# Modulation in eight contraction chunks, with seven projection blocks run on each chunk and their sums kept in SBUF, in a one-step hybrid decoder layer

## The reference, cut to what matters

```python
mod = c @ w_ada + b_ada                      # w_ada: 4096 x 12288
shift, scale, gate = jnp.split(mod, 3, axis=-1)
h = _rmsnorm(x, g_norm) * (1.0 + scale[:, None]) + shift[:, None]
proj = h @ w_in                              # w_in: 4096 x 10240
a_b, a_c, a_x, a_g, b_x, b_g, c_u, c_g = _split_cols(proj)
# A: gated convolution of 3, B: convolution of 4 and RG-LRU, C: complex S5, GELU and GLU
mixed = jnp.concatenate([out_a, out_b, out_c], axis=-1) @ w_out
x = x + gate[:, None] * mixed                # then a final RMSNorm of x
```

## Time and profile before

| what | us |
|---|---|
| median of 3 runs | 2138.58 (2137.79 to 2139.91) |
| the profiled execution | 2137.69 |
| its span, first to last instruction | 2136.1 |
| TensorE busy | 2007.3 (94%) |
| VectorE, ScalarE, POOL busy | 1051.4, 800.7, 434.3 |
| mean granted TensorE clock | 0.986 of 2.4 GHz |
| read from HBM, written | 463.09 MB, 10.07 MB |

### The profile page before, as it was taken

How to read it: one execution, slowest core, us unless ns; L and a number is a source line. 1 busy time by engine, 2 the same in 40 slices (tenths; PEclk the granted TensorE clock), 3 DMA queues, 4 the chain that set the end, 5 groups by cost and what they waited for, 6 DMA issues and landing times.

```text
span 2136.1 us, 36787 instructions
## 1 busy us (share of the span) xinstructions
PE 2007.3 (94%) x13066; PEld 1724.2 (81%) x13066; DVE 1051.4 (49%) x1324; ACT 800.7 (37%) x1075; POOL 434.3 (20%) x501
## 2 busy tenths in 40 slices
PE   2887999999999998999989999999999999999994
PEld 0111777778999997989979999999988888888883
DVE  4812233233447677676777455565653333333334
ACT  3001223233334444444435445646563323333232
POOL 0000000000107765867658101000000000000001
PEclk9999999999999999999999999999999999999997
DMA  7999999997543433334333444454457787666862
GB/s 311 410 410 385 334 339 348 344 332 291 172 144 127 133 127 117 129 120 141 123 126 130 161 147 165 134 173 154 155 216 259 261 318 258 249 247 246 306 234 98
DMA packets 129149, 473.88 MB, mean 222 GB/s; under 512 B 14640, under 2 KB 15472, under 8 KB 128960
## 3 DMA queue, kind: packets, MB, share of 16 engines
q1 hardware_dynamic: 122256, 445.70, 58.1%
q0 software_dynamic: 4816, 18.10, 2.5%
q10 hardware_dynamic: 2016, 9.42, 1.1%
HBM read 463.09 MB, written 10.07 MB: 222 GB/s over the span
## 4 chain that ended last, share of the span: by engine, by line
PE 74%; POOL 7%; DMA 7%; issue 5%; DVE 4%; ACTq 1%; ACT 1%; POOLq 0%; SPq 0%; DVEq 0%
PE m L375 22%; PE m L377 21%; PE m L376 21%; DMA ada_ring<-in_ada 6%; PE aux L393 4%; PE aux L499 3%; POOL s_tmpp L1260 1%; POOL s_tmpp L1257 1%; PE aux L481 1%; DVE x L1184 1%; POOL cos L1218 1%; POOL s_h__105 L1256 1%; POOL sin L1216 1%; DMA ada_ring_x<-in_ada 1%; DVE w_lo L833 1%
## 5 line engine op out<-in xcount | busy, mean ns | idle before, releaser
L375 PE MATMUL m<-h_hi,w_hi 128*128 128x320 f32 x3584 | 1131.8, 316 | 4.7 <-DVE w_lo L833 4.6
L377 PE MATMUL m<-h_hi,w_lo 128*128 128x320 f32 x3584 | 1109.4, 310 | 0.0
L376 PE MATMUL m<-h_lo,w_hi 128*128 128x320 f32 x3584 | 1109.0, 309 | 0.0
L833 DVE TENSOR_TENSOR w_lo<-w_raw,w_hi 128x1024 fp32r<-128x1024 f32 x456 | 577.4, 1278 | 838.4 <-ACT w_hi L529 837.3
L529 ACT ACTIVATE w_hi<-w_raw 128x1024 fp32r<-128x1024 f32 x456 | 478.9, 1056 | 903.2 <-PE m L377 577.5
L375 PEld LDWEIGHTS m<-h_hi,w_hi 128*128 128x128 f32 x3584 | 674.9, 188 | 130.9 <-issue 113.6
L376 PEld LDWEIGHTS m<-h_lo,w_hi 128*128 128x128 f32 x3584 | 675.5, 188 | 0.8
L377 PEld LDWEIGHTS m<-h_hi,w_lo 128*128 128x128 f32 x3584 | 675.0, 188 | 0.0
L393 PE MATMUL aux<-ada_ring,c_T 128*32 128x512 f32 x512 | 123.8, 620 | 24.3 <-DMA ada_ring<-in_ada 24.3
L393 PEld LDWEIGHTS aux<-ada_ring,c_T 128*32 128x32 f32 x512 | 17.7, 110 | 124.2 <-DMA ada_ring<-in_ada 120.1
L393 PE MATMUL aux<-ada_ring_x,c_T 128*32 128x512 f32 x512 | 70.8, 612 | 3.6 <-DMA ada_ring_x<-in_ada 3.6
(11 more groups left out here) (237 smaller groups left out, 1507.6 us busy)
## 6 DMA issues: line engine op xcount, KB each, us to landing
w_raw<-in_w SPq DMA_DIRECT2D x456, 512.0 KB, 4.3
ada_ring<-in_ada SPq DMA_DIRECT2D x128, 512.0 KB, 9.0
ada_ring_x<-in_ada SPq DMA_DIRECT2D x128, 512.0 KB, 5.9
gate_ring<-in_ada SPq DMA_DIRECT2D x128, 512.0 KB, 5.7
x<-in_x ACTq DMA_DIRECT2D x1, 5120.0 KB, 16.6
x<-in_x POOLq DMA_DIRECT2D x8, 640.0 KB, 5.3
out_y<-x SPq DMA_DIRECT2D x7, 640.0 KB, 3.0
part_b<-part_b POOLq DMA_DIRECT2D x4, 688.0 KB, 6.5
```

The lines of the kernel that those rows point to most:

```text
L375: mm(out, w_hi, hi[:, k, :], start=k == k0, stop=False)
L376: mm(out, w_hi, lo[:, k, :], start=False, stop=False)
L377: last = mm(out, w_lo, hi[:, k, :], start=False, stop=k == k0 + nk - 1)
L833: tt(W_LO[:, c % RING], RAW[:, c % RING].rearrange("p (k n) -> p k n", k=2), W_HI[:, c % RING].bitcast(F32), SUB).then_inc(w_lo_done, 1)
```

## The change

What it does:

- `w_ada` is stored by contraction tile of h: nine chunks of 32 slabs. A slab of a chunk holds one contraction tile of c by 4 x 256 columns. Chunks 0 to 7 carry shift and scale for four contraction tiles of h each; chunk 8 and three later double chunks carry the gate, each for two output groups. Four calls per slab, one per quarter of the array's columns, 256 columns moving; all 32 contraction tiles accumulate in the same place, so nothing is left to add. VectorE's 32 x 32 transpose turns the result (`turned`); `SEL` and its matmuls go.
- x is loaded in eight pieces and scaled in place (`XH`).
- The head: seven blocks (b_x 0 to 2 and the four c blocks), 14 half blocks of 256 columns, eight chunks of h: 112 slabs (`head_slab`), each four contraction tiles by 256 columns, 24 matmuls in two banks of `M`, the two pairs of banks in turn. After each head slab TensorE takes one pair of modulation slabs (at two of 14 places two pairs) for the next chunk. On chunk 0 ScalarE writes the sums to SBUF (`first_sums`), afterwards VectorE adds to them (`sums`). Only the three b_x blocks go to HBM.
- The S5 preparation is done in four batches between the head slabs of the first four chunks.
- A and the GLU stay. B: three b_g groups, then b_x 3 and b_g 3, 16 slabs each.
- Output: the gate's last 96 slabs are taken in pairs of groups; the last group is read from its banks directly by VectorE; ScalarE multiplies x by `g_final` group by group, and the tail is one multiplication on VectorE.

The diff, cut (of replaced parts only the new side is shown, but for the constants):

```diff
@@ -40,23 +40,27 @@
 SPG = KT // 2
 AHEAD = 3
 RING = 4
-SPH = SPG // 2
 SPGG = W_C // P // 2
-N_P, N_U, N_A, N_G, N_B, N_O = 8, 4, 8, 2, 8, 8
-SLAB_U = N_P * SPH
-SLAB_A = SLAB_U + N_U * SPH
+HC, HK = 256, 4
+HGROUPS, HSTEPS = 7, 8
+HSL = 2 * HGROUPS
+N_H = HSL * HSTEPS
+N_A, N_G, N_O = 8, 2, 8
+SLAB_A = N_H
 SLAB_G = SLAB_A + N_A * SPG
 SLAB_B = SLAB_G + N_G * SPGG
-SPB = SPH + SPG
-SLAB_O = SLAB_B + N_B // 2 * SPB
+SLAB_O = SLAB_B + 5 * SPG
 SLABS = SLAB_O + N_O * SPG
-Q_U = N_P
-Q_A = Q_U + N_U
+Q_A = 0
 Q_G = Q_A + N_A
 Q_B = Q_G + N_G
-Q_O = Q_B + N_B
-ADA_J = 8
-ADA_1 = ADA_J // 2
+Q_O = Q_B + 5
...
+        def head_place(n):
+            g, half = n % HSL // 2, slice(2 * (n % 2), 2 * (n % 2) + 2)
+            if g < 3:
+                return BX[g][:, half, 0:TP], BXS[g][:, half, :, 3:]
+            tiles = slice(4 * ((g - 3) % 2) + half.start, 4 * ((g - 3) % 2) + half.stop)
+            if g < 5:
+                return CST[:, tiles, 0:TP], CSTS[:, tiles, :, 1:]
+            return SG[:, tiles, 0:TP], SGS[:, tiles, :, 1:]
+        pairs_after = {n: [q for q in range(128) if q * HSL // 16 - 3 == n] for n in range(-3, N_H)}
+        def ada_place(n):
+            if n < KT:
+                return n % 6, n // 6 + 1, n - 5
+            m = n % RING
+            first = KT + m
+            return m, len(range(m, KT, 6)) + (n - first) // RING + 1, (
+                n - RING + 1 if n >= first + RING else max(range(m, KT, 6)) + 1)
+        FIN = [(0, 0, 2), (0, 2, 4)] + [(g, 0, 4) for g in range(1, 7)] + [(7, 0, 2), (7, 2, 4)]
...
+            for n in range(24):
+                ada_in(n)
             for n in range(RING):
+                w_in(n)
+            for n in range(24, KT + RING):
+                ada_in(n)
+            s5_batch(0)
+            for n in range(-3, N_H):
+                if n in (HSL - 2, 2 * HSL - 2, 3 * HSL - 2):
+                    s5_batch((n + 2) // HSL)
+                for q in pairs_after[n]:
+                    for m in (KT + RING + 2 * q, KT + RING + 2 * q + 1):
+                        if m < CHUNKS * KT:
+                            ada_in(m)
+                if RING <= n + 6 < N_H:
+                    w_in(n + 6)
...
+            def ada_slab(n, bank):
+                slot, landed, _ = ada_place(n)
+                pe.wait_ge(ada_landed[slot], 16 * landed)
+                k = n % KT
+                for r in range(4):
+                    last = mm(A0[bank][32 * r:32 * r + 32, 0:CW], CT[:, k, :], ADAX[slot][:, r, :], start=k == 0,
+                              stop=k == KT - 1)
+                last.then_inc(ada_used, 1)
+            def pairs(n):
+                for q in pairs_after[n]:
+                    j = 1 + q // 16
+                    if q % 16 == 0 and j >= 2:
+                        pe.wait_ge(mod_done, j - 1)
+                    for m in (KT + 2 * q, KT + 2 * q + 1):
+                        ada_slab(m, j % 2)
+            def head_slab(n):
+                st_, l, s_ = n // HSL, n % HSL, n % RING
+                pe.wait_ge(w_lo_done, n + 1)
+                if l == 0:
+                    pe.wait_ge(h_lo_done, st_ + 1 + 1)
+                if 2 <= n < HSL + 2:
+                    pe.wait_ge(hda_free, n - 2 + 1)
+                if n >= HSL + 2:
+                    pe.wait_ge(hdv_free, n - 2 - HSL + 1)
+                for b in range(2):
+                    out = M[:, 2 * (n % 2) + b, 0:T]
+                    for kk in range(HK):
+                        k = HK * st_ + kk
+                        at_ = kk % 2 * HC + b * P
+                        w_hi = W_HI[:, s_, kk // 2, at_:at_ + P]
+                        w_lo = W_LO[:, s_, kk // 2, at_:at_ + P]
+                        mm(out, w_hi, H_HI[:, k, :], start=kk == 0, stop=False)
+                        mm(out, w_hi, H_LO[:, k, :], start=False, stop=False)
+                        last = mm(out, w_lo, H_HI[:, k, :], start=False, stop=kk == HK - 1)
+                last.then_inc(slab_done, 1)
+            pe.wait_ge(c_in, 16)
+            for n in range(24):
+                ada_slab(n, 0)
             pe.wait_ge(sqa_done, 8)
             for i in range(4):
+                last = mm(A0[3][:, 0:T], ONES[:], SQA[:, i * T:(i + 1) * T], start=i == 0, stop=i == 3)
             last.then_inc(sum_done, 1)
+            for n in range(24, KT):
+                ada_slab(n, 0)
+            for n in range(-3, 0):
+                pairs(n)
...
+            def group_o(j):
                 for c in range(SPG):
                     if c % 2 == 0:
                         pe.wait_ge(mix_lo_done, c // 2 + 1)
                     slab(SLAB_O + j * SPG, c, KT, Q_O + j, H_HI, H_LO, T)
+                    yield c
...
+            with pe.Fori(0, 3) as p:
+                k = 0
+                pe.wait_ge(gmod_done, p + 1 + 1)
+                for jj in range(2):
+                    for c in group_o(2 * p + jj):
+                        if c not in ((1, 3, 5, 7, 9, 11, 13, 15) if jj else (2, 4, 6, 8, 10, 12, 14, 15)):
+                            continue
+                        for k in (k, k + 1):
+                            pe.wait_ge(gate_landed[k % RING], 128 * p + 16 * (k // RING + 1))
+                            for r in range(4):
+                                last = mm(A0[0][32 * r:32 * r + 32, 0:CW], CT[:, k, :], ADA2[:, k % RING, r, :],
+                                          start=k == 0, stop=k == KT - 1)
+                            last.then_inc(gate_used, 1)
+                        k += 1
...
+            def first_sums(n):
+                if n == 0:
+                    act.wait_ge(acc_clear, 5)
+                act.wait_ge(slab_done, n + 1 + 1)
+                row, few = head_place(n)
+                bk = 2 * (n % 2)
+                fn(row, M[:, bk:bk + 2, 0:TP], ACT.Copy)
+                fn(few, MS[:, bk:bk + 2], ACT.Copy).then_inc(hda_free, 1)
...
+            def norm_weight(j):
+                for b in range(BLK):
+                    fn(X[:, 4 * j + b, :], X[:, 4 * j + b, :], ACT.Copy,
+                       scale=PAR[:, bass.ds(C_GF + 4 * j + b, 1)]).then_inc(gf_done, 1)
...
+            def turned(dst, j):
+                dve.wait_ge(ada_used, KT * (j + 1))
+                nc.vector.transpose(dst[:].rearrange("p b n -> p (b n)"), A0[j % 2][:, 0:CW]).then_inc(mod_done, 1)
+                dve.wait_ge(mod_done, j + 1)
+            def h_rows(j):
+                turned(MODT, j)
+                bias = PAR[:, C_BADA:C_BADA + 64].rearrange("p (s k) -> p s k", s=2)[:, :, 4 * j:4 * j + 4]
+                then(tt(MOD[:], MODT[:, :, 0:9].rearrange("p (s b) n -> p s b n", s=2),
+                        bias.unsqueeze(3).to_broadcast([P, 2, BLK, 9]), ADD))
+                then(tt(MOD[:, 1], MOD[:, 1], bias9(C_G + 4 * j), MUL))
+                for kk in range(BLK):
+                    row = XH[:, 4 * j + kk, 0:TP]
+                    ts(row, row, MOD[:, 1, kk, 0:1], MOD[:, 0, kk, 0:1], MUL, ADD)
+                few = XHS[:, 4 * j:4 * j + 4]
+                then(tt(few, few, MOD[:, 1, :, 1:9].unsqueeze(3).to_broadcast([P, BLK, DB, DS]), MUL))
+                tt(few, few, MOD[:, 0, :, 1:9].unsqueeze(3).to_broadcast([P, BLK, DB, DS]), ADD).then_inc(ht_done, 1)
+            def h_lo(j):
+                dve.wait_ge(h_hi_done, j + 1 + 1)
+                tt(H_LO[:, 4 * j:4 * j + 4, :], XH[:, 4 * j:4 * j + 4, :], H_HI[:, 4 * j:4 * j + 4, :].bitcast(F32),
+                   SUB).then_inc(h_lo_done, 1)
+            def sums(n):
+                dve.wait_ge(slab_done, n + 1 + 1)
+                if n < 2 * HSL:
+                    dve.wait_ge(hda_free, n - HSL + 1)
+                else:
+                    dve.wait_ge(hdv_free, n - 2 * HSL + 1)
+                row, few = head_place(n)
+                bk = 2 * (n % 2)
+                tt(row, row, M[:, bk:bk + 2, 0:TP], ADD)
+                tt(few, few, MS[:, bk:bk + 2], ADD).then_inc(hdv_free, 1)
...
+            x_scale(0)
+            for n in range(AHEAD):
+                lo(0, n)
+            h_rows(0)
+            h_lo(0)
+            for n in range(N_H):
+                st_, l = n // HSL, n % HSL
+                if n > HSL:
+                    sums(n - 1)
+                if l == 12 and st_ < HSTEPS - 1:
+                    h_lo(st_ + 1)
+                lo(0, n + AHEAD)
+                if n < HSTEPS - 1:
+                    x_scale(n + 1)
...
+            with dve.Fori(0, 3) as p:
+                st.enter(p, 2)
+                for odd in range(2):
+                    group_o(2 * p + odd, odd, False)
+                dve.wait_ge(gate_used, KT * (p + 1))
+                nc.vector.transpose(MODT2[:].rearrange("p b n -> p (b n)"), A0[0][:, 0:CW]).then_inc(gate_t_done, 1)
+                dve.wait_ge(gate_t_done, p + 1)
+                tt(MODG[:], MODT2[:, :, 0:9], PAR[:, bass.ds(C_BADA + 72 + 8 * p, 8)].unsqueeze(2).to_broadcast(
+                    [P, 8, 9]), ADD).then_inc(gmod_done, 1)
+            st.leave(3)
```

(44 more changed lines are left out.)

827 lines of the change are left out of this document (364 added, 463 removed).

## The result

The changed kernel takes 2116.78 us (median of 4 runs, 2114.26 to 2118.77) against 2138.47 for the kernel before (2137.79 to 2139.91): a ratio of 0.9897, 95% interval 0.988 to 0.9914. So it is faster by 1.0%, as forecast in sign, but by 22 us where 74 were forecast, and outside the range of 2045 to 2105. The profiled execution took 2118.8 us, its span 2117.2.

The account below looks back on a forecast made before the run. The kernel was taken as a transfer-bound prologue of 211 us, then a TensorE-bound rest. Terms -132 + 52 - 3 + 5 - 14 + 8 + 18 - 8 = -74 took 2137.7 to 2064 us; range 2045 to 2105.

Parts of the forecast that it names:

- Part 1: Prologue: the head needs one chunk of h, so it starts at 79 us instead of 211: -132 us.
- Part 2: Modulation pairs move from the prologue to TensorE's bound: +44 x 1.19 = +52 us; 16 back-to-back pairs save 3.
- Part 3: Modulation pair's new form, eight calls of 256 columns: +5 us, 9 by the skill's overhead; bounds 0 and 26.
- Part 4: The selecting matmuls go, VectorE's transpose replaces them, hidden: -14 us.
- Part 5: Head sums kept in SBUF by VectorE, under the 4.7 us period: hidden, cost 0.
- The wait for hdv_free: Sign of a wrong forecast: a head slab waits for hdv_free.
- The prediction's other sign of being wrong: Stage A starting after 660 us, where about 630 was expected.
- Part 6: Head transfers: four-slot ring costs 0.5 us at each of 16 doubled places, +8 us; bounds 0 and 45.
- transfers set the head's pace: Rival, chance 0.20: head stalls at both pairs after 16 places, 32 us, 2088 us; to 2105 with a 339 GB/s ceiling.
- the start at 87 us: Head start estimated from the skill's 358 GB/s for one core, instead of 79 us; the forecast did not adopt it.
- Part 7: Output stage: two added TensorE waits for gmod_done, 7.2 us each, 8.9 with clock loss: +18 us, between 13 and 20.
- Part 8: Tail: last group's banks read straight from PSUM and shorter final scaling: -8 us, between -5 and -11.

Follow-up runs that it names:

- experiment 11: Experiment 7's kernel with a fifth slot in the head's modulation ring, serving up to the 237th slab: 2055.8 us, 0.9612 of the kernel before.
- experiment 7: Experiment 3's kernel with the first batch of S5 loads issued by SP just ahead of the head's slab 0: 2075.1 us, 0.9716 of the kernel before.
- experiment 6: Changed kernel with only half of each modulation slab transferred from the 37th on, all instructions kept: 2081.4 us, head 539.3 us.
- experiment 5: Changed kernel with the w_hi by h_lo product left out of the head, transfers unchanged: 2050.8 us, head 509.0 us.
- experiment 2: Changed kernel with the gate's modulation pairs early in their output groups, as in the kernel before: 2091.3 us, 0.9776 of the kernel before.
- experiment 3: Changed kernel with the gate's pairs early and TensorE waiting for gmod_done only before a double group's first modulation pair: 2077.6 us, 0.9716 of the kernel before.
- experiment 4: Changed kernel with the head's modulation slabs shared out singly, two or three behind each weight slab: 2118.7 us, 0.9905 of the kernel before.
- experiment 10: Experiment 7's kernel with head weight loads issued earlier, ahead of the modulation loads, and modulation slabs shared out singly: 2079.9 us, 0.9726 of the kernel before.

## Why the prediction was wrong

**Part 1, the start: 84.2 us instead of 79.** The count of bytes holds only if the loads run on without a break. After the 32nd slab the ring shrinks from six slots to four, and TensorE waits 10.6 us for slabs between 60 and 85 us, 3.5 at the longest. With five slots (experiment 11) the head starts at 77.4, so the term was right for a ring that doesn't limit. The cause that I first gave the late start, the S5 batch on SP, fell with experiment 7.

**Parts 2 to 5.** The single pairs cost the 1.19 us that the prediction took; a second pair costs 0.87 where 1.0 was counted, and the new form 0 where +5 was, and up to +9 by its other estimate. By experiment 6 the head without stalls is 539.3 us, where the prediction's own sum, less its 8 for transfers, gives 543. Everything called hidden there was hidden. The wait for hdv_free that would have shown otherwise appears nowhere. The prediction's other sign of being wrong did appear: stage A started at 661.0 us, where 660 was the limit named.

**Part 6 is the step that failed in the head:** +8 us taken, 37.6 measured, inside its bounds of 0 to 45. The mechanism was named and even its numbers were there (5.3 us from issue to use at a doubled place, 5.9 us to land), but the price was taken as their difference, 0.5 us. Two things were left out. The median landing time is no bound, since a slab of the doubled place is issued behind what is still queued: the pair issued from 251.40 on was waited for until 257.1 and 258.3. And the second slab can be used 1.24 us after the first, so both are waited for, and the next place starts late too: ten places behind doubled ones lost 7.6 us. The rival "transfers set the head's pace" priced this nearer (32 us), with stalls at both pairs behind a doubled place, but gave a wrong reason for its upper end: 339 to 341 GB/s is no ceiling of the transfers (382 in experiment 5) but what four slots bring at 6 us a landing.

On that point the Trainium skill ("DMA: Bandwidth & Descriptors", Anatomy of one DMA) puts a fixed cost of about 2.0 us on each transfer beside its bytes at 436 GB/s, for the path through GpSimd. For 512 KB that gives 3.2 us, an estimate. In stage A, where a weight slab is asked for once in some 4 us, the load takes 3.3 us in the median; the trace agrees, though SP issues it:

```profile
w_raw<-in_w SPq DMA_DIRECT2D x118, 512.0 KB, 3.3
```

The same page of the Trainium skill (Specifications) gets its 358 GB/s for one core by dividing a stack's rate between two. Here one core was at work, and the 382 GB/s of experiment 5 over 300 us exceed it; the start at 87 us that the prediction estimated from it was undercut too, by 84.2 and, with five slots, 77.4.

**Part 7, the output stage: +25 us over a forecast that held 18 for waiting.** The wait itself was right: 7.2 us worked out, 7.2 measured once the weights are on time (experiment 2). What failed is that the change of places for the gate's pairs was never walked through SP's queue. The prediction counted the 16 pairs fewer and did not ask what stands behind the pairs at a group's last slabs. That is ScalarE's weight copies, then the emptying of the banks, then TensorE: three waits of 5 us, 3.4 for w_lo, 1.7 more on each of the two forecast waits, and the clock at 0.50 behind each. Experiments 2 and 3 give these back.

**Part 8, the tail:** 22.4 us instead of 25; the last bank's chain took 2.61 us of waiting at the sum over partitions instead of 5.94, and the scaling 11.4 instead of 16.0.

**The gain, then.** The head starts 127 us earlier and the tail is 10 shorter. Of these 137 us, 38 were given back to the ring of four in the head and 39 to waits in the output stage, and 19 are left, the difference of the two spans; the other 41 are, by subtraction, TensorE work that moved out from beside the prologue's transfers (parts 2 to 4 gave 40). With the repairs and a fifth slot the time falls by 61 us (2116.8 to 2055.8); in the profiled run 7 us of its gain are an earlier start, the rest is waiting that comes back. What is left in the head of version 11 is 17 us over the 539.3 of experiment 6. Most of it lies where four slots serve: 9.9 us behind the 237th slab, of which 5.3 are one place where a period takes 10.9 instead of 5.58 us (11.1 in the changed kernel, behind POOL's writes of part_b at 600.27 and 609.70). That those writes cause it was not tried.

## What to carry to other kernels

Price a prefetch ring by its depth, not by the mean rate: for each place in the order, set the time from the issue of a slab to its use (the use of the slab that held its slot) against the landing time with what is queued in front, and add a further 1.28 us for each slab more in the same place. One slot less costs at every place where that difference changes sign (665 us for 573); sharing the same slabs out more evenly gave nothing (experiments 4 and 10). When an order is shifted on one queue, walk every load that stands behind it through to the engine that ends a group. Two edits of a few lines, waiting only where the bank is written and taking the pairs early, gave back nearly twice what the whole change had won.

## What the runs showed of the hardware

Packets of one size do not all take the same time. For a packet of 4 KB 159 ns was the commonest time in every stage counted. In the changed kernel's head (200 to 500 us) 6.8% of them took over 200 ns, 460 in the mean; in the prologue before (45 to 195 us) it was 0.4%, in experiment 5 between 200 and 300 us 1.5%. In the head the time of these slow packets beyond 159 ns is a tenth of the engines' time, which is how a share of 0.94 goes with 341 GB/s and one of 1.02 with 398 and 406. What makes a packet slow is not shown. In stage A, where for half of the time none was under way, 16.7% were slow; but the 100 us of experiment 5 had fewer than five under way for longer (3.1% of the time) than the changed kernel's head (1.0%), and fewer slow ones.

Two rounds of 32-column products at 256 columns, 16 matmuls in a pair, took the time of eight at 512 columns to within 0.05 us: the doubled number of instructions and weight loads did not show.
